# Weights stationary for the x, B and C columns of two hybrid layers

## The reference, cut to what matters

```python
proj = h @ w_in                                   # h: 256 x 1024, already normed
q, k, v, z, xbc, dt = jnp.split(proj, [Q_END, K_END, V_END, Z_END, XBC_END], axis=-1)
...
xbc = jax.nn.silu(causal_depthwise_conv(xbc, conv_w, conv_b))     # 1536 channels, 4 taps along the rows
xs, bm, cm = jnp.split(xbc, [SSM_INNER, SSM_INNER + SSM_GROUPS * D_STATE], axis=-1)
...
y = ssd_chunked(xs, dt, a_neg, bm, cm) + d_skip[:, None] * xs
```

## Time and profile before

| | us |
|---|---|
| median of three runs (855.89 to 856.34) | 856.08 |
| the profiled execution | 856.24 |
| its span, first to last instruction | 854.4 |
| PE busy | 846.6 (99%) |
| DVE busy | 627.3 (73%) |
| ACT busy | 534.5 (63%) |
| POOL busy | 202.8 (24%) |

### The profile page before, as it was taken

How to read it: one execution, slowest core, us unless ns; L and a number is a source line. 1 busy time by engine, 2 the same in 40 slices (tenths; PEclk the granted TensorE clock), 3 DMA queues, 4 the chain that set the end, 5 groups by cost and what they waited for, 6 DMA issues and landing times.

```text
span 854.4 us, 13034 instructions
## 1 busy us (share of the span) xinstructions
PE 846.6 (99%) x4645; PEld 708.3 (83%) x4645; DVE 627.3 (73%) x1125; ACT 534.5 (63%) x1031; POOL 202.8 (24%) x176
## 2 busy tenths in 40 slices
PE   9999999999999999999999999999999999999996
PEld 7877888778887888888888888887888888888885
DVE  6867866778776797688888546576797688888544
ACT  8668466866897864655565434797874655665432
POOL 0212053110152430043333000152330043334001
PEclk9999999999999999999999999999999999999998
DMA  9814553445534346666565555444346566655631
GB/s 323 288 56 134 177 201 128 149 148 178 164 131 148 124 132 213 189 201 185 190 197 184 211 197 176 150 147 147 103 146 221 175 199 195 191 181 179 233 104 50
DMA packets 94308, 146.21 MB, mean 171 GB/s; under 512 B 5924, under 2 KB 54564, under 8 KB 94244
## 3 DMA queue, kind: packets, MB, share of 16 engines
q1 hardware_dynamic: 92212, 139.58, 49.9%
q0 software_dynamic: 1296, 4.72, 1.6%
q10 hardware_dynamic: 736, 1.07, 0.3%
HBM read 144.32 MB, written 1.05 MB: 170 GB/s over the span
## 4 chain that ended last, share of the span: by engine, by line
PE 99%; issue 0%; POOL 0%; DVE 0%; ACT 0%; POOLq 0%; DVEq 0%
PE bank L1362 58%; PE bank L1316 17%; PE bank L1318 9%; PE bank L1243 6%; PE bank L1519 2%; PE bank L1447 1%; PE bank L1423 1%; PE bank L1420 1%; PE bank L1450 1%; PE bank L1248 0%; PE bank L1259 0%; PE bank L1262 0%; PE bank L1264 0%; PE bank L1509 0%; PE bank L1526 0%; PE bank L1487 0%
## 5 line engine op out<-in xcount | busy, mean ns | idle before, releaser
L1152 DVE TENSOR_TENSOR lo<-raw,hi 128x1024 fp32r<-128x1024 f32 x242 | 309.5, 1296 | 103.6 <-ACT hi L1538 103.2
L1538 ACT ACTIVATE hi<-raw 128x1024 fp32r<-128x1024 f32 (+1 forms) x258 | 269.5, 1061 | 140.7 <-PE bank L1362 68.9
L1362 PE MATMUL bank<-hi,xT 128*128 128x512 f32 (+2 forms) x800 | 251.9, 386 | 0.0
L1362 PEld LDWEIGHTS bank<-hi,xT 128*128 128x128 f32 x800 | 147.2, 188 | 30.8 <-issue 4.3
L1316 PE MATMUL bank<-xT,hi 128*128 128x512 f32 x640 | 153.1, 391 | 0.0
L1362 PE MATMUL bank<-lo,xT 128*128 128x512 f32 (+2 forms) x400 | 151.0, 378 | 0.0
L1316 PEld LDWEIGHTS bank<-xT,hi 128*128 128x128 f32 x640 | 117.5, 188 | 23.3 <-DVE quarter L2127 0.6
L1362 PE MATMUL bank<-hi,hT 128*128 128x512 f32 x348 | 107.8, 389 | 0.0
L1362 PEld LDWEIGHTS bank<-lo,xT 128*128 128x128 f32 x400 | 75.4, 189 | 12.1
L1318 PEld LDWEIGHTS bank<-xT,lo 128*128 128x128 f32 x640 | 81.9, 191 | 3.0
L1318 PE MATMUL bank<-xT,lo 128*128 128x256 f32 x640 | 83.2, 283 | 0.0
(11 more groups left out here) (284 smaller groups left out, 1116.2 us busy)
## 6 DMA issues: line engine op xcount, KB each, us to landing
raw<-in_w_in SPq DMA_DIRECT2D x26, 1024.0 KB, 5.1
raw<-in_w_down SPq DMA_DIRECT2D x22, 1024.0 KB, 5.0
raw<-in_w_out SPq DMA_DIRECT2D x20, 1024.0 KB, 5.0
raw<-in_w_gate SPq DMA_DIRECT2D x20, 1024.0 KB, 5.3
raw<-in_w_up SPq DMA_DIRECT2D x20, 1024.0 KB, 5.3
raw<-in_w_in_b SPq DMA_DIRECT2D x10, 1024.0 KB, 5.0
raw<-in_w_in_a SPq DMA_DIRECT2D x7, 1024.0 KB, 8.0
raw<-in_w_in_a SPq DMA_DIRECT2D x8, 256.0 KB, 5.7
```

The lines of the kernel that those rows point to most:

```text
L1152: return engine.tensor_tensor(lo[r][:, cols], raw[c.i % RAW][:, cols], hi[r][:, cols].bitcast(F32), ALU.subtract)
L1362: last = nc.tensor.matmul(bank[:, 0:wd], still[a], mv[r][:, off:off + wd], start=c.first and i == 0 and j == 0, stop=(c.last or c.closes a ...
L1538: nc.scalar.activation(hi[c.i % SPLIT][:, cols], raw[c.i % RAW][:, cols], ACT.Copy)\
```

## The change

The 1536 channels are projected by `weights_still` in six blocks of 256 columns (`x_columns(j, u)`), one chunk each. `x_tiles(j, u)` brings each to SBUF in two steps `x_tile`: ScalarE copies one half out of PSUM into `low`, VectorE adds the other half from PSUM and writes `x0` or `x1`, and GpSimd multiplies that in place by `row_scale`, the norm factor of each row. `x_scale` makes `row_scale` once a layer with two transposes. The `conv` steps lose their transposes and read SBUF; so do their `scalar_tensor_tensor`, whose inputs now both lie in SBUF. `xin`, `ev_x` and the `ended(pe, s.ev, ...)` of the transposes are gone. The number of chunks, their size and `pool_splits` stay; a DMA row of these chunks is 256 columns long and not 512.

```diff
--- before.py
+++ after.py
@@ -596,18 +596,30 @@
     def att(*ns):
         return [lambda n=n: attention(sc, n) for n in ns]
 
+    def x_columns(j, u, beside=(), after=()):
+
+        b = scan["block", j, u] = sc.block(512)
+        c0 = x0 + (SSM if j == 0 else (j - 1) * 512) + 256 * u
+        sc.weights_still([(KD * 256, (w_in, c0, 256, list(range(KD))))], [(b, 0, 0), (b, 1, P)], list(range(KD)),
+                         beside, after)
+
+    def x_tiles(j, u):
+
+        b = scan["block", j, u]
+        b["evac"] = [sc.step("x_tile", j=j, u=u, q=i, block=b, of=scan["scale"]) for i in range(2)]
+        scan["tiles", j, u] = b["evac"][1]
+
+    def x_scale():
+        bk = sc.bank()
+        scan["scale"] = sc.step("x_scale", bank=bk, rstd=sc.rstd)
+        bk.freed = (scan["scale"], "scalar")
+
     def conv(j, u):
-        bk = sc.bank()
-        s = sc.step("conv", j=j, u=u, bank=bk, ev=scan["ev", j], layer=layer,
-                    conv=scan["silu", j - 1] if j else None)
-        bk.freed = (s, "vector")
-        scan["conv", j] = s
+        scan["conv", j] = sc.step("conv", j=j, u=u, of=scan["tiles", j, u], layer=layer,
+                                  conv=scan["silu", j - 1] if j else None)
 
     def conv_silu(j):
         scan["silu", j] = sc.step("conv_silu", j=j, layer=layer, conv=scan["conv", j])
-
-    def evac_x(b, j):
-        scan["ev", j] = evacs(sc, b, "ev_x", j=j, conv=scan["conv", j - 1] if j else None)
 
     def back(j):
         b1, b2 = sc.bank(), sc.bank()
@@ -691,24 +703,21 @@
 
 
     sc.low_later = True
-    b = halves(sc, w_in, [(x0 + SSM, 512)], do(turn_queries, sc, a, 0, rq) + do(soft, 1),
-               do(turn_keys, sc, a, kr) + do(soft, 2), att(0) + do(soft, 3))
-    evac_x(b, 0)
+    x_columns(0, 0, do(x_scale) + do(turn_queries, sc, a, 0, rq) + do(soft, 1), do(turn_keys, sc, a, kr) + do(soft, 2))
+    x_columns(0, 1, do(x_tiles, 0, 0) + att(0) + do(soft, 3))
 
     next_chunk = sc.count["chunk"]
     for i in range(POOL_SPLITS):
         if i in POOL_BOTH:
             sc.pool_splits.append((next_chunk + i, 0))
         sc.pool_splits.append((next_chunk + i, 1))
-    b = halves(sc, w_in, [(x0, 512)], do(norm_probs, sc, a, "scalar", 0, 4) + do(sums), att(1),
-               do(norm_probs, sc, a, "vector", 4, 2) + do(conv, 0, 0))
-    sc.goes_on(do(conv, 0, 1) + do(norm_probs, sc, a, "vector", 6, 2))
-    evac_x(b, 1)
-    b = halves(sc, w_in, [(x0 + 512, 512)], do(conv_silu, 0), att(2) + do(conv, 1, 0), do(conv, 1, 1))
-    evac_x(b, 2)
-    sc.goes_on(att(3))
+    x_columns(1, 0, do(x_tiles, 0, 1) + do(norm_probs, sc, a, "scalar", 0, 4) + do(sums), att(1))
+    x_columns(1, 1, do(x_tiles, 1, 0) + do(norm_probs, sc, a, "vector", 4, 2) + do(conv, 0, 0),
+              do(conv, 0, 1) + do(norm_probs, sc, a, "vector", 6, 2))
+    x_columns(2, 0, do(x_tiles, 1, 1) + do(conv_silu, 0), att(2) + do(conv, 1, 0))
+    x_columns(2, 1, do(x_tiles, 2, 0) + do(conv, 1, 1), att(3))
     scan["gain"] = sc.gain(("ssm_norm", layer))
-    b = halves(sc, w_in, [(z0, 512)], do(conv_silu, 1), do(conv, 2, 0) + do(bback),
+    b = halves(sc, w_in, [(z0, 512)], do(x_tiles, 2, 1) + do(conv_silu, 1), do(conv, 2, 0) + do(bback),
                do(back, 0) + do(conv, 2, 1))
     scan["z", 0] = evacs(sc, b, "ev_z", j=0, kind_of="h")
     sc.goes_on(do(conv_silu, 2))
...
@@ -1303,7 +1316,10 @@
                 for n, (b, m, col) in enumerate(c.outs):
-                    if half == 0 and b["before"]:
+                    if half == 0 and b["lent"][m]:
+                        step, who = b["lent"][m].freed
+                        ended(pe, step, who)
+                    elif half == 0 and b["before"]:
                         e = b["before"]["evac"][m]
...
@@ -1469,14 +1485,6 @@
                 last.then_inc(sem["sums", "tensor"], 1)
-            elif s.kind == "conv":
-                ended(pe, s.ev, "scalar")
-                bank = freed(pe, s.bank)
-                for i in range(2):
-                    for m in range(M):
-                        c0 = (2 * s.u + i) * P
-                        last = transpose(bank[:, (2 * i + m) * P:(2 * i + m + 1) * P], Hb["xin"][:, m, c0:c0 + P])
-                last.then_inc(sem["conv", "tensor"], 1)
...
@@ -1645,12 +1653,14 @@
                 done(nc.scalar.activation(z, z, ACT.Silu), s)
-            elif s.kind == "ev_x":
-                bank = ready(act, s.block, s.m)
-                if s.conv is not None:
-                    ended(act, s.conv, "tensor")
-                done(nc.scalar.activation(Hb["xin"][:, s.m, :], bank[:, :], ACT.Copy,
-                                          scale=rms[:, 1, s.m:s.m + 1]), s)
+            elif s.kind == "x_scale":
+                ended(act, s, "tensor")
+                done(nc.scalar.activation(Hb["row_scale"][:, :], psum[4 + s.bank.at][:, 0:S], ACT.Copy), s)
+            elif s.kind == "x_tile":
+                bank = ready(act, s.block, s.q)
+                if s.i >= 2:
+                    act.wait_ge(sem["x_tile", "vector"], s.i - 1)
...
@@ -1769,12 +1779,12 @@
 
-                act.wait_ge(sem["conv", "tensor"], s.i + 1)
+                ended(act, s.of, "gpsimd")
                 if s.conv is not None:
                     ended(act, s.conv, "scalar")
                 for i in range(2):
                     ct = 2 * s.u + i + (8 if s.j == 0 else 4 * (s.j - 1))
-                    last = nc.scalar.activation(Hb[f"acc{s.u}"][:, i, :], psum[4 + s.bank.at][:, i * S:(i + 1) * S],
+                    last = nc.scalar.activation(Hb[f"acc{s.u}"][:, i, :], Hb[f"x{s.j % 2}"][:, 2 * s.u + i, :],
...
@@ -1841,6 +1851,11 @@
                   .then_inc(sem[s.kind, "gpsimd"], 1)
+            if s.kind == "x_tile":
+                ended(pool, s.of, "scalar")
+                ended(pool, s, "vector")
+                x = Hb[f"x{s.j % 2}"][:, 2 * s.u + s.q, :]
+                nc.gpsimd.tensor_tensor(x, x, Hb["row_scale"][:, :], ALU.mult).then_inc(sem["x_tile", "gpsimd"], 1)
             if s.kind == "mid_load":
...
@@ -2272,14 +2288,18 @@
                 done(copy(csum[64:96, :, :], left[64:96]), s)
+            elif s.kind == "x_tile":
+                ended(dve, s, "scalar")
+                done(tt(Hb[f"x{s.j % 2}"][:, 2 * s.u + s.q, :], psum[2 * s.block["pair"] + s.q][:, 0:S],
+                        Hb[f"low{s.i % 2}"][:, :], ALU.add), s)
             elif s.kind == "conv":
 
                 dve.wait_ge(sem["conv", "scalar"], s.i + 1)
-                cw, bank = convw[:, s.layer, :, :], psum[4 + s.bank.at]
+                cw, tiles = convw[:, s.layer, :, :], Hb[f"x{s.j % 2}"]
                 for tap in range(1, 4):
                     for i in range(2):
                         ct = 2 * s.u + i + (8 if s.j == 0 else 4 * (s.j - 1))
-                        acc, x = Hb[f"acc{s.u}"][:, i, :], bank[:, i * S:(i + 1) * S]
+                        acc, x = Hb[f"acc{s.u}"][:, i, :], tiles[:, 2 * s.u + i, :]
                         if tap > 1:
```

More of the change, by code:

```diff
@@ L908 @@
     "taps": ("tensor", "scalar"), "mid_gain": ("vector",), "square": ("scalar",), "row_square": ("scalar",), "meansq": ("vector", "gpsimd"), "newton": ("vector",), "added": ("vector",),
-    "ev_kv": ("scalar",), "ev_q": ("scalar",), "ev_z": ("scalar",), "z_silu": ("scalar",), "ev_x": ("scalar",),
+    "ev_kv": ("scalar",), "ev_q": ("scalar",), "ev_z": ("scalar",), "z_silu": ("scalar",), "x_tile": ("scalar", "vector", "gpsimd"), "x_scale": ("tensor", "scalar"),
     "ev_up": ("scalar", "vector"), "rows": ("tensor", "scalar"),
@@ L919 @@
     "soft1": ("vector", "scalar"), "soft2": ("vector", "scalar"), "soft3": ("vector",),
-    "sums": ("tensor", "vector", "scalar"), "conv": ("tensor", "scalar", "vector"), "conv_silu": ("scalar",),
+    "sums": ("tensor", "vector", "scalar"), "conv": ("scalar", "vector"), "conv_silu": ("scalar",),
     "bback": ("tensor", "scalar", "vector"), "xback": ("tensor", "scalar", "gpsimd"),
@@ L925 @@
 }
-BLOCK_BY_VECTOR = "added", "ev_up", "f_gate", "f_up"
+BLOCK_BY_VECTOR = "added", "ev_up", "f_gate", "f_up", "x_tile"
 def build(nc, t):
@@ L1057, in plan @@
             small_at = put("cross", [P, 2, P], where=e)
-            put("xin", [P, M, 512])
+            put("x0", [P, 4, S])
             put("cT", [P, NCT, S])
@@ L1070, in plan @@
             put("xg", [P, M, SSM])
+            e = put("row_scale", [P, S], where=b["xg_at"])
+            for i in range(2):
+                e = put(f"low{i}", [P, S], where=e)
+            put("x1", [P, 4, S], where=b["xg_at"] + 4 * SSM)
             e = rope_at
@@ L1378, in _ @@
                 last.then_inc(sem["turn", "tensor"], 1)
-            elif s.kind == "rows":
+            elif s.kind in ("rows", "x_scale"):
                 ended(pe, s.rstd, "vector")
@@ L1383, in _ @@
                     last = transpose(bank[:, m * P:(m + 1) * P], spread(rms[:, 1, m:m + 1], [P, P]))
-                last.then_inc(sem["rows", "tensor"], 1)
+                last.then_inc(sem[s.kind, "tensor"], 1)
```

(10 more changed lines are left out.)

## The result

| | median, us (lowest to highest) | runs |
|---|---|---|
| before | 855.99 (855.74 to 856.34) | 4 |
| after | 872.70 (871.65 to 872.99) | 4 |

The ratio is 1.0193, 95% interval 1.0181 to 1.0205: 16.7 us slower, where 873 was forecast. The profiled execution after took 871.65 us with a span of 869.9, 15.5 more than before.

What follows compares the result with a forecast made beforehand. TensorE was 99% of the chain of waits. Later steps, mainly turns between VectorE and GpSimd, delay `diag` by 8.5 us a layer, +17 on 856.24: 873 us. Forecast 868 to 876 (55%); 857 to 879 holds about 8 in 10.

Steps and rivals of the forecast that it cites:

- The lock: Convolution taps with two SBUF inputs take turns with GpSimd's operations, one by one; in full, 8.1 us more a layer.
- "probably" on `p_norm_vector`: VectorE's normalizing of heads probably takes turns with GpSimd too; 128 columns more cost only 69 ns.
- no-lock: Rival: convolution taps take no turns with GpSimd, only the early waits stay against the saving; 857 us, 13%.
- the faster rival: Rival: early waits are absorbed and the turns fail too, so only the saving of 3.2 us stays; 853 us, 7%.
- Half of it: Rival: turns occur, but VectorE's gaps take up more, leaving about half of 8.1 us a layer; 864 us, 17%.
- One sign: In the profile after, GpSimd's splits would take above 2.4 us more often.
- `diag` was over-estimated: First hybrid: the `diag` matmuls start at 301.2 instead of 292.67, 8.5 us later, after a 3.0 us wait.
- behind `diag` I take no further loss: After the `diag` matmuls all engines are shifted alike, so a layer's loss stays at 8.5 us.
- the second flip group: TensorE needs heads 6 and 7 at 261.75 and waits 2.8 us; its next chunk starts at 265.6, 3.9 later.
- The clock rival: Waits near 3 us a layer halve TensorE's clock for a stretch, costing 6 us in all; 879 us, 8%.
- The saving on TensorE: Transposes dropped from the convolution, less costs of chunks and `x_scale`, save 1.6 us a layer, 3.2 for both.
- The early waits: TensorE waits about 0.9 us for normalizing heads 0 to 3, and 1.1 for lent banks behind the scores.

Runs made afterwards that it cites:

- e1: Changed kernel with the convolution's running sums in a scratch PSUM bank, so each tap has one SBUF and one PSUM operand: 863.66 us.
- e4: Kernel before, with ScalarE copying the turned x from PSUM to SBUF and the convolution's taps reading that copy: 867.77 us.
- e2: Changed kernel with the scaling of x by the row's factor done by VectorE, not GpSimd: 887.38 us.
- e5: e1 with heads 4 to 7 normalized by ScalarE, not VectorE: 858.52 us.
- e12: e5 reordered: normalizing of heads 0 to 3, sums, then x tiles; block 1's first-half convolution after block 2's first x tiles: 856.99 us.
- e6: e5 with heads 0 to 3 normalized ahead of ScalarE's copies for the second x block, and one lent bank less: 862.67 us.
- e7: Changed kernel with heads 0 to 3 normalized ahead of ScalarE's x copies and one lent bank less, running sums in SBUF: 877.45 us.
- e9: e5 with heads 0 to 3 normalized one step earlier and the sums moved behind the scores of attention(sc, 1): 860.19 us.

## Why the prediction was right

| step, first hybrid | forecast | measured |
|---|---|---|
| heads 0 to 3 normalized; PE's wait | 244.3; 0.9 | 244.7; 1.1 |
| chunk behind the scores; wait for the lent bank | 248.5; 1.1 | 249.05; 1.2 |
| heads 4 and 5; heads 6 and 7 normalized | 258.6; 264.5 | 258.7; 264.6 |
| wait for them; next chunk | 2.8; 265.6 | 2.2; 265.49 |
| x_tile(2,0) | 273.2 | 272.9 |
| z's second chunk; wait | 280.6; 0.8 | 280.22; 0.5 |
| conv(2,1) ends | 294.1 | 292.9 |
| second z block; wait | 295.3; 2.0 | 294.22; 0.95 |
| second weighing ends | 301.1 | 299.9 |
| first `diag`; wait | 301.2; 3.0 | 298.94; 1.7 |
| loss of the layer | 8.5 | 8.2, the second 7.7 |

**The lock** is the mechanism: e1 takes it from the taps and gets 9.0 us, e4 puts it into the kernel before and loses 11.8. The Trainium skill, SBUF — State Buffer, "Who interferes with whom", says that an operation of VectorE with two SBUF inputs and a GpSimd instruction that reads SBUF exclude each other for a whole instruction, and one with at most one SBUF input and outside the two-port modes does not contend; `tensor_scalar` it names among those that can enter such a mode. The traces agree in both halves: 2614 ns against 489, and in e2 2.11 against 0.41 us beside the same split. The normalizing is a `tensor_scalar` with one input in SBUF, and it took turns too, 2503 ns; that it runs in such a mode is inferred from its rate, as in the prediction, and no run isolates it. The prediction's "probably" on `p_norm_vector` is thus shown, and with e5 worth 5.1 us with what follows it.

**The no-lock and the faster rival** fall with these rows. **Half of it** falls too: 8.2 and 7.7 us a layer are nearly all of the 8.5. One sign failed: POOL's splits are not above 2.4 us more often (8 of 16 in both kernels). It was VectorE that stood for the splits.

**Two steps were off, and that they cancelled is luck.** First, `diag` was over-estimated: it starts 6.3 late, not 8.5. Conv(2,1) began 0.5 earlier and took 5.59 us, not 6.3: three products of `back` were passed and not four, the second having gone ahead of it (POOL, 286.42). That makes the second weighing 1.2 earlier. And `diag` starts behind the first weighing, 1.0 ahead of the second's end; its second half waits 0.1 for that. Second, "behind `diag` I take no further loss" was wrong: VectorE is 8.2 us late there (the second weighing starts at 299.22, before at 291.02) and TensorE only 6.3, so TensorE meets VectorE's lateness further on. In the second layer 0.9 us go in the wait for `hyb_xs`, a scratch bank that the join on VectorE, itself taking turns (1.28 us at 304.69 in the first layer), frees late. In the first layer the clock fell. With `diag` 6.3 late and nothing behind it, the sum would have been 856.24 + 12.6 = 868.8: the mechanism and the range would stand, the hit within 0.3 us would not. A slip of 0.1 is in the prediction's sum for the second flip group, 261.65 and not 261.75.

**The clock rival** was partly true, in one layer. The page's row of tenths hides it (all 9). TensorE in stretches of 2 us, kernel after (stretch, its length, PE busy, matmuls, mean granted clock, DMA share, GB/s):

```profile
296.00:298.00 2.00, 1.22 (x6) 1.00 0.78 188
298.00:300.00 2.00, 1.06 (x9) 1.00 0.87 336
300.00:302.00 2.00, 2.00 (x13) 0.63 0.03 8
302.00:304.00 2.00, 2.00 (x9) 0.52 0.00 0
304.00:306.00 2.00, 2.00 (x11) 1.00 0.39 35
```

The granted clock is 1.2 GHz, half of 2.4, for about 3.4 us (1.5 of the third stretch and 1.9 of the fourth), behind waits of 0.95 us up to 294.22 and 1.72 up to 298.94. The price can be read off one group, the timeline of PE after, against 1.04 us before for the same eight transposes:

```profile
301.26 1.92 PE L1256 MATMUL bank<-cst,hyb_cT 128*128 128x128 f32 x8
```

From `back`'s transposes at 301.26 (before 294.39) to the decays at 306.19 (before 298.03) the loss grows from 6.9 to 8.2, so 1.3 us. The last four matmuls of `diag`, ahead of that, take 0.79 us and not 0.45, which makes 1.6, about half of the 3.4. Not all of it is net: in the second layer, where the clock stayed, TensorE came earlier and waited the 0.9 for `hyb_xs`, and the loss is 7.7, only 0.5 less than in the first. I gave the clock 6 us with 8%; it took 1.6 at most in the profiled run. The other three runs, 0.8 to 1.3 us longer, have a mean clock of 0.990 to 0.992 and not 0.996. In e2, with waits of 5.7, it falls three times a layer, for 3.4 to 6.8 us each, some 27 us in all at half speed, so 13.5 us lost: e2's span is 32.1 longer and its waits are 23.4, which leaves 4.8 for TensorE's saving. e1's four runs go from 861.21 us at 0.999 to 864.91 at 0.993, the same kernel.

**The saving on TensorE** was 1.6 a layer in the forecast. In e12 the matmuls ahead of the first hybrid start 0.4 us earlier than before and the last one 1.0 later, so its two hybrids take 1.5 more, with 5.4 of waits where there were none: 4.0 us saved, 2.0 a layer. A wait costs more than its row, though: in e4, where TensorE has the work of before, eight waits of 10.0 us in all go with a loss of 11.5. At 0.2 more for each, e12 comes to 2.4 a layer. So the forecast saving was 0.4 to 0.8 too low. A small part of it is the 0.11 more a chunk: the chunk at 254.67 lasts to 260.32, that of before from 252.62 to 258.27, 5.65 us both, of which 0.08 before belong to the transposes; so it is 0.08 or less. The rest stays open.

**The early waits** came as forecast, 1.1 and 1.2. Whether they are worth 2.3 a layer stays open too: e6, e7 and e9 replaced them, e12 got back 1.5 us in all, with another edit in it.
